# Attention inside a two-block transformer kernel: the order of the score and value products of a pair of heads

## What is computed

```python
# l in 0..1; h = rms_norm(x); proj = h @ w_in[l]; heads of 64 wide, queries in blocks of 128
# differential attention: 4 heads, each of two halves m = 0, 1 with values 128 wide
logits = einsum('bqhmd,bkhmd->bhmqk', qi, k) * scale, causal
p = softmax(logits);  p = p[:, :, 0] - lam * p[:, :, 1]
o = einsum('bhqk,bkhe->bqhe', p, v)
# forgetting attention: 8 heads with values 64 wide
decay = c_i - c_k                      # c = cumsum(log sigmoid(forget logits))
logits = einsum('bqhd,bkhd->bhqk', qi, k) * scale + decay, causal
p = softmax(logits);  o = einsum('bhqk,bkhd->bqhd', p, v)
# x = x + rms_norm(concat(o) @ w_out[l]); then the gated feed-forward network
```

## Time and profile before

| | |
|---|---|
| median of three runs | 2915.88 us |
| the profiled execution's own time | 2914.42 us |
| its span | 2912.3 us |
| PE, weight loads, DVE, ACT busy | 96%, 74%, 55%, 40% |
| attention of layer 0 (pairs 0 to 7) | 64.7 to 340 us of the span |

### The profile page before, as it was taken

One profiled execution on the slowest core, in us unless ns is written; L12 is line 12 of the kernel. 1 busy time (PEld: TensorE's weight loads), 2 busy tenths in 40 slices (PEclk: granted clock), 3 DMA queues, 4 the chain that ended last, 5 costly groups with the idle time before them and its releaser, 6 DMA issues.

```text
span 2912.3 us, 38409 instructions
## 1 busy us (share of the span) xinstructions
PE 2797.6 (96%) x12473; PEld 2168.3 (74%) x12473; DVE 1598.5 (55%) x2511; ACT 1152.9 (40%) x1848; POOL 83.3 (3%) x87
## 2 busy tenths in 40 slices
PE   6999989999799998999989999999999999999999
PEld 4666768888566666888856776888888887788887
DVE  5653465544565346554465555554447888554442
ACT  3333344433333334443345555322225666432222
POOL 3000010000200001000010000000000000000000
PEclk8999999999799999999999999999999999899999
DMA  3111123333211112333321110333332222133333
GB/s 95 52 44 44 55 68 98 97 94 92 68 44 51 44 41 68 99 96 94 97 66 46 44 50 29 95 100 94 97 96 82 59 58 58 51 98 97 94 100 94
DMA packets 417199, 214.81 MB, mean 74 GB/s; under 512 B 6747, under 2 KB 415942, under 8 KB 417094
## 3 DMA queue, kind: packets, MB, share of 16 engines
q1 hardware_dynamic: 416144, 212.89, 25.2%
q10 hardware_dynamic: 950, 0.58, 0.1%
HBM read 211.34 MB, written 2.10 MB: 73 GB/s over the span
## 4 chain that ended last, share of the span: by engine, by line
issue 50%; PE 43%; DVE 3%; POOL 2%; ACT 1%; DMA 0%; DVEq 0%; POOLq 0%; ACTq 0%; SPq 0%
PE acc L608 35%; PE sc L1002 2%; POOL yT L568 1%; PE sc L859 1%; PE sc L843 1%; PE po L872 1%; PE po L905 1%; PE aux L898 0%; PE tp L843 0%; PE tp L859 0%; PE po L1025 0%; PE po L1022 0%; DVE w_lo L1164 0%; DVE xT L1282 0%; PE sc L991 0%
## 5 line engine op out<-in xcount | busy, mean ns | idle before, releaser
L608 PE MATMUL acc<-h_hi,w_hi 128*128 128x512 f32 x2048 | 840.5, 410 | 63.4 <-DVE h_lo L1097 46.9
L608 PE MATMUL acc<-h_hi,w_lo 128*128 128x512 f32 x2048 | 805.3, 393 | 0.0
L608 PE MATMUL acc<-h_lo,w_hi 128*128 128x512 f32 x2048 | 804.1, 393 | 0.0
L1694 ACT ACTIVATE w_hi<-w_raw 128x1024 fp32r<-128x1024 f32 x398 | 420.8, 1058 | 751.8 <-PE acc L608 748.8
L1164 DVE TENSOR_TENSOR w_lo<-w_raw,w_hi 128x1024 fp32r<-128x1024 f32 x398 | 486.2, 1222 | 77.2 <-ACT w_hi L1694 75.7
L608 PEld LDWEIGHTS acc<-h_hi,w_hi 128*128 128x128 f32 x2048 | 387.8, 189 | 176.6 <-DVE h_lo L1097 58.0
L608 PEld LDWEIGHTS acc<-h_hi,w_lo 128*128 128x128 f32 x2048 | 387.6, 189 | 84.1
L608 PE MATMUL acc<-mid_hi,w_hi 128*128 128x512 f32 x1120 | 440.8, 394 | 5.5 <-DVE mid_lo L1615 3.2
L608 PEld LDWEIGHTS acc<-h_lo,w_hi 128*128 128x128 f32 x2048 | 388.8, 190 | 74.4 <-issue 5.1
L608 PE MATMUL acc<-mid_lo,w_hi 128*128 128x512 f32 x1120 | 439.6, 393 | 0.0
L608 PE MATMUL acc<-mid_hi,w_lo 128*128 128x512 f32 x1120 | 439.5, 392 | 0.0
(11 more groups left out here) (306 smaller groups left out, 2744.2 us busy)
## 6 DMA issues: line engine op xcount, KB each, us to landing
w_raw<-in_mlp_w_dram SPq DMA_DIRECT2D x128, 512.0 KB, 4.1
w_raw<-in_w_in_dram SPq DMA_DIRECT2D x48, 512.0 KB, 3.8
w_raw<-in_w_gate_dram SPq DMA_DIRECT2D x44, 512.0 KB, 3.7
w_raw<-in_w_up_dram SPq DMA_DIRECT2D x44, 512.0 KB, 3.7
w_raw<-in_w_down_dram SPq DMA_DIRECT2D x32, 512.0 KB, 4.1
w_raw<-in_hg_w_in_dram SPq DMA_DIRECT2D x32, 512.0 KB, 4.0
w_raw<-in_sb_w_qkv_dram SPq DMA_DIRECT2D x24, 512.0 KB, 3.8
w_raw<-in_w_out_dram SPq DMA_DIRECT2D x16, 512.0 KB, 4.2
```

Source lines behind the costliest of these rows:

```text
L608: mm = pe.matmul(bank[:], w[:, k], r[:, k], start=(k == 0 and i == 0), stop=(k == k_tiles - 1 and i == 2))
L1694: ACTV(w_hi[:, slot], w_raw[:, slot], ACT.Copy).then_inc(w_rounded, 1)
```

## The change

`score` for one head becomes `scores(p, t)` for both. It runs in the even slots 0, 2, 4, 6. Both products of queries and keys are issued first, then (forget-gate pairs) the first decay product of both heads, the second of both, then both masks. It waits once, for both exponentials of the block before. DVE's and ACT's programs for maxima and exponentials stay as they are, one per slot.

In forget-gate pairs the transposes of both heads of a block are issued one behind the other in slots 3, 5, 7 and 9, and ACT takes them there. The value products of a block are one group, `pv_heads(p, t)`, in slots 5, 7, 9 and 10, ahead of that slot's transposes. In it the two heads alternate, block of keys by block of keys. Differential pairs keep their transposes and value products. Number, size and operands of all products stay the same.

```diff
-                def score(p, s):
-                    t, m = s // 2, s % 2
-                    bank, n = sc[s % 2], (t + 1) * P
-                    if s == 0:
+                def scores(p, t):
+                    n = (t + 1) * P
+                    if t == 0:
...
-                    if p * 8 + s >= 2:
-                        pe.wait_ge(exp_done, l * 64 + p * 8 + s - 1)
-                    r = slice(HD * m, HD * m + HD)
-                    pe.matmul(bank[:, 0:n], qT[p % 2][r, t * P:t * P + P], kT[p % 2][r, 0:n], start=True, stop=False)
+                    if p * 4 + t >= 1:
+                        pe.wait_ge(exp_done, l * 64 + p * 8 + 2 * t)
+                    for m in range(2):
+                        r = slice(HD * m, HD * m + HD)
+                        pe.matmul(sc[m][:, 0:n], qT[p % 2][r, t * P:t * P + P], kT[p % 2][r, 0:n], start=True, stop=False)
                     if p >= NDIFF:
-                        h = 2 * (p - NDIFF) + m
                         for i in range(2):
-                            pe.matmul(bank[:, 0:n], sel_r[96:128, h, :], decay_r[96:128, i, 0:n], start=False, stop=False)
-                    pe.matmul(bank[:, t * P:n], ident_r[:], mask_r[:], start=False, stop=True).then_inc(score_done, 1)
+                            for m in range(2):
+                                h = 2 * (p - NDIFF) + m
+                                pe.matmul(sc[m][:, 0:n], sel_r[96:128, h, :], decay_r[96:128, i, 0:n], start=False, stop=False)
+                    for m in range(2):
+                        pe.matmul(sc[m][:, t * P:n], ident_r[:], mask_r[:], start=False, stop=True).then_inc(score_done, 1)
...
+                def pv_heads(p, t):
+                    ti = T_BASE[p] + 2 * t
+                    if t == 0:
+                        pv_may_start(p)
+                    pe.wait_ge(t_taken, l * T_BASE[PAIRS] + ti + 2)
                     for j in range(t + 1):
-                        mm = pe.matmul(po[r, t * P:t * P + P], vtok[:, j, r], probT[ti % 2][:, j * P:j * P + P],
-                                       start=(j == 0), stop=(j == t))
-                    mm.then_inc(pv_done, 1)
+                        for m in range(2):
+                            r = slice(HD * m, HD * m + HD)
+                            mm = pe.matmul(po[r, t * P:t * P + P], vtok[:, j, r], probT[m][:, j * P:j * P + P],
+                                           start=(j == 0), stop=(j == t))
+                    mm.then_inc(pv_done, 2)
...
-                        if p >= 0 and k < 8:
-                            score(p, k)
+                        if p >= 0 and k < 8 and k % 2 == 0:
+                            scores(p, k // 2)
...
                         elif p >= NDIFF:
-                            if 2 <= k < 10:
+                            for t in range(NB):
+                                if k == min(2 * t + 5, SLOTS - 2):
+                                    pv_heads(p, t)
+                            if k in (3, 5, 7, 9):
+                                transpose_p(p, k - 3)
                                 transpose_p(p, k - 2)
-                            if 3 <= k < 11:
-                                pv(p, k - 3)
...
-                        if p >= NDIFF and 2 <= k < 10:
+                        if p >= NDIFF and k in (3, 5, 7, 9):
+                            take_t(p, k - 3)
                             take_t(p, k - 2)
```

More of the change, by code:

```diff
@@ L730, in pv, with pv_may_start @@
                     ti = T_BASE[p] + i
-                    t = i if p < NDIFF else i // 2
-                    r = slice(0, P) if p < NDIFF else slice(HD * (i % 2), HD * (i % 2) + HD)
                     if i == 0:
-                        pe.wait_ge(aux_free, A + AUX[("v", p)] + 1)
-                        if p >= 1:
-                            pe.wait_ge(po_taken, l * PAIRS + p)
+                        pv_may_start(p)
                     pe.wait_ge(t_taken, l * T_BASE[PAIRS] + ti + 1)
-                    for j in range(t + 1):
-                        mm = pe.matmul(po[r, t * P:t * P + P], vtok[:, j, r], probT[ti % 2][:, j * P:j * P + P],
-                                       start=(j == 0), stop=(j == t))
-                    mm.then_inc(pv_done, 1)
+                    for j in range(i + 1):
+                        mm = pe.matmul(po[:, i * P:i * P + P], vtok[:, j], probT[ti % 2][:, j * P:j * P + P],
+                                       start=(j == 0), stop=(j == i))
+                    mm.then_inc(pv_done, 1)
+                def pv_heads(p, t):
+                    ti = T_BASE[p] + 2 * t
+                    if t == 0:
+                        pv_may_start(p)
+                    pe.wait_ge(t_taken, l * T_BASE[PAIRS] + ti + 2)
+                    for j in range(t + 1):
+                        for m in range(2):
[3 more added lines that the diff above has]
+                    mm.then_inc(pv_done, 2)
+                def pv_may_start(p):
+                    pe.wait_ge(aux_free, A + AUX[("v", p)] + 1)
+                    if p >= 1:
+                        pe.wait_ge(po_taken, l * PAIRS + p)
                 def use_aux(name):
```

## The result

| | before | after |
|---|---|---|
| median | 2915.9 us (4 runs) | 2843.8 us (4 runs, 2842.4 to 2845.1) |
| ratio after / before | | 0.974, 95% interval 0.9719 to 0.9761 |
| the profiled execution | 2914.4 us | 2845.1 us |

The kernel became 72 us faster. Forecast were 54 us, 2862 us, and a range that ended at 2847. The direction, the saved switches and the places of the new waits were right; how the two heads' products overlap was not, and the gain was larger than what I had taken for its upper bound. Before itself takes 2913 to 2918 us in most of its runs and about 2925 in the others, which have a mean granted clock of 0.975 instead of about 0.978, and one execution of `e3_values_only`, 10736.65 us, stands apart from all others and was not profiled.

What follows compares the result with a forecast made beforehand. Attention was taken to be bound by TensorE (PE), some 550 of 2912 us. 2914.4 - 38.0 (switches) - 30.8 (overlap) + 15 (waits) = 2860.6, 2862 us on the median; range 2847 to 2895.

Steps and rivals of the forecast that it cites:

- What bounds it: Attention, some 275 us per layer: bound by PE, so each microsecond saved there shortens the kernel until a wait replaces it.
- Switches of shape: Scores back to back save 2.4 us per forget-gate pair, 1.6 per differential; grouped value products 0.75 per forget-gate pair; 38.0 total.
- Overlap: Two heads' score and value products: saves 0 to 30.8 us (17.1 scores, 13.7 values); the upper end was taken.
- The added wait: Scores of a block wait for both exponentials of the block before: 7.3 us per layer, mostly pairs 0 to 3 and 7.
- The sum again: Whole kernel: 2914.4 less 38.0 switches, less 30.8 overlap, plus 15 waits gives 2860.6, 2862 us on the median.
- Serial: Rival: the two heads' products on different halves don't overlap; 2891 us, 2892 on the median; chance 0.18.
- overlap of one kind alone: Rival: only rows (scores) or only columns (value products) overlap; 2875 or 2878 us; chance 0.14.
- draining halves: Rival: changing half within one shape drains the array, 192 changes at 0.21, 40 us; 2931 us, slower; chance 0.06.
- The chain's waits: Rival: DVE's chain from first to second maximum adds 0.5 us at each of 48 blocks, 24 us; serial 2915; chance 0.10.

Runs made afterwards that it cites:

- e3_values_only: Before, with paired transposes and alternating value products of both heads, but one score per slot as before; 2902.5 us (0.994).
- E5: After, with VectorE taking both maxima of a block in the even slot, ahead of that slot's other passes; 2824.7 us (0.967).
- e1: Before, with the scores of both heads back to back, transposes and value products as before; 2866.8 us (0.983).
- e2: As e1, but both heads' products of queries and keys use rows 0 to 63, so they can't overlap; 2911.9 us (0.997).
- e6: After, but value products of both heads go to partitions 0 to 63 and are summed there, so they can't overlap; 2860.1 us.
- e4: After, but in a block's value products head 0 has all its blocks of keys first, then head 1; 2847.6 us.
- e9: e5, with head 0's decay in forget-gate pairs read from a copy on rows 32 to 63, head 1 still on 96 to 127; 2820.3 us (0.967).
- e7: After, but in pair 7 42 instead of 30 ordinary products fill the 18 slots; 2846.7 us.
- e8: After, with the changes of e5 and e7 together; 2830.1 us.

## Why the prediction was too small

- **What bounds it.** Right. Attention was bound by TensorE; savings of PE's time came out at the end but for the added waits, and little else moved.
- **Switches of shape.** Right. E5, in which PE waits in none of the pairs compared, shows them best: 31.25 - 27.57 = 3.68 us in a differential pair, less 2.10 of overlap, leaves 1.58 (forecast 1.6); 37.87 - 30.59 = 7.28 in a forget-gate pair, less 2.14 and 2.16 of overlap, leaves 2.98 (forecast 2.4 + 0.75 = 3.15). Over all pairs that is an estimated 36.5 us for the 38.0. E3's 2.90 less the 2.16 bears out the 0.75 of the value products.
- **Overlap.** This is the step that failed. "The second instruction of one head can run beside the first of the other", so "of a score block's four instructions one is hidden", was called the upper bound. It took for granted, without a row for it, that TensorE keeps the order of issue across both halves. Two of four are hidden: 2.13 us per pair instead of 1.07 for the scores (e1 against e2) and 2.1 instead of 1.7 for the value products (e3, e6). Over 16 and 8 pairs it is 34.1 + 17.1 = 51 us where the sum had 30.8. What the runs showed in place of the kept order: a half begins its products without waiting for those issued before them for the other half, over about four of them (e4). The trace of before could not tell it, since no two such products are neighbours there; the true bound from it would have been that the second head costs nothing, and the range should have begun there.
- **The added wait.** Right in mechanism, place and size: 7.1 us per layer for the exponentials against 7.0, and e5 took nearly all of it away by moving one maximum. In pair 7 two things came on top: 0.5 us more of waits for the copies, and the lower clock, 2.7 us in layer 1. The 1.0 us per layer that PE no longer waits at pair 1 goes the other way.
- **The sum again.** With the switches as measured, the overlap, the waits for exponentials and copies, the wait that went, and the clock: 2914.4 - 36.5 - 51.2 + 14.2 + 1.6 - 2.0 + 2.7 = 2843.2; the profiled execution took 2845.1. The low end of the range, 2847, was the overlap as I had bounded it with hardly a wait.
- **The rivals.** Serial is refuted by e1 against e2, overlap of one kind alone by that pair (rows) and by e6 against after (columns), draining halves by the 0.01 us between two heads' products. The chain's waits did not reach all 48 blocks.

## What to carry to other kernels

Put products that use different halves of TensorE's rows or columns, or different quarters of its rows, side by side. Here the second one was free, and a run of the same shape saved some 0.1 to 0.2 us for each change of shape. The products on different rows wrote different banks here; one bank for both was not tried. With more than about four instructions per part, alternate them. When that makes one wait stand for two results, move what the second result needs to the front of the other engine's slot (here one maximum, 19 us), and before filling a wait with other products look at what those products cover where they are.

## What the runs showed of the hardware

- Products on disjoint halves start within 0.01 us of each other although the first half's second instruction was issued in between, in rows (L710, 64 rows) and columns (L751, 64 columns); two on different quarters (L719 of e9, 32 rows, neighbours in the program) do so too. The Trainium skill ("TensorEngine Tiling (Array Packing)", Key Properties) says that different tiles can run weight loads and matmuls in parallel; for the matmuls this case now shows it (1.06 us for both heads' L710 on 512 keys, 1.91 on the same rows). The Trainium skill ("TensorE: Matmul & The Clock Gate", Part 3: Packing small matmuls — row/col tiling) says that matmuls start and end in program order. The traces don't agree as to the starts; ends are modelled. In after, head 0's second L710 comes before head 1's first in the program, yet head 1's first starts with head 0's first. Clearer still is e4, in which all of head 0's L751 of a block stand ahead of head 1's first. A cut of 0.15 us through its timeline of PE, at the second block of a pair (four instructions per head), shows two L751 started; one alone lasts 0.32 us, so both start within 0.02 us:

```profile
230.29 0.34 PE L751 MATMUL po<-scratch,yT 128*64 128x128 f32 x2
```

- The early start reaches over about four queued product instructions of the other half, measured on 128 columns: nothing lost with 4 per head, 0.27 us with 6, 0.49 with 8.
- The granted clock fell to the 1.2 GHz level inside pair 7 in five of the eleven kernels (after, e2, e3, e4, e6), and just behind it, where PE had waited 3.4 us for weights, in e7 and e8; it did not in before, e1, e5 and e9. This is what one profiled execution of each shows, two of after. In e2 it fell in pair 0 as well. In after the place is the same in two executions: 0.53 over 984.8 to 992, behind a stretch with waits; the same waits in pair 7 of layer 0 were followed by no fall. In e3 it fell behind 15.1 us in which PE was busy without a gap, though mostly with products on part of the array and few ordinary ones between. So waits alone don't explain it; what does was not settled.
